# Prompt attention in pairs of heads on the halves of the matmul array, with half of the output projection between the units

## What is computed

```python
def _sparse_attend(q, ks, vs, valid):
    logits = jnp.einsum('bqhd,bqkhd->bqhk', q, ks).astype(jnp.float32) * (ATT_DIM ** -0.5)
    logits = jnp.where(valid[:, :, None, :], logits, -jnp.inf)
    p = jax.nn.softmax(logits, axis=-1).astype(vs.dtype)
    return jnp.einsum('bqhk,bqkhd->bqhd', p, vs)
...
    y = jnp.concatenate([att.reshape(B, T, ATT_WIDTH), jax.nn.silu(g) * retn], axis=-1)
    return y @ w_out
```

## Time and profile before

| | |
|---|---|
| median of 3 runs | 1618.3 us (1616.56 to 1624.8) |
| profiled execution | 1621.1 us, its span 1619.3 us |
| PE busy | 1528.2 us, 94% of the span |
| DVE, ACT, POOL busy | 567.3, 427.7, 193.3 us |
| mean granted clock of TensorE | 0.922 of 2.4 GHz |

### The profile page before, as it was taken

How to read it: one execution, slowest core, us unless ns; L and a number is a source line. 1 busy time by engine, 2 the same in 40 slices (tenths; PEclk the granted TensorE clock), 3 DMA queues, 4 the chain that set the end, 5 groups by cost and what they waited for, 6 DMA issues and landing times.

```text
span 1619.3 us, 27331 instructions
## 1 busy us (share of the span) xinstructions
PE 1528.2 (94%) x10150; PEld 1275.8 (79%) x10150; DVE 567.3 (35%) x1102; ACT 427.7 (26%) x686; POOL 193.3 (12%) x309
## 2 busy tenths in 40 slices
PE   6999999999999999999887689999989999999995
PEld 6999999999876477777532365556869999999995
DVE  3233333222412589802122354431153332332224
ACT  3334333221312200003110003331073343332123
POOL 0000000233131022220242110000140000000001
PEclk9999999999999999999998755557999999999998
DMA  4222222333222388873677420000202222222231
GB/s 185 79 91 79 90 80 88 89 105 96 75 70 93 110 257 256 260 247 126 196 254 243 126 104 1 0 1 27 78 28 90 91 83 86 91 87 72 84 94 56
DMA packets 65352, 176.76 MB, mean 109 GB/s; under 512 B 9682, under 2 KB 13779, under 8 KB 65043
## 3 DMA queue, kind: packets, MB, share of 16 engines
q1 hardware_dynamic: 49874, 131.30, 25.5%
q0 software_dynamic: 14560, 40.96, 8.0%
q10 hardware_dynamic: 864, 3.80, 0.6%
HBM read 169.00 MB, written 7.02 MB: 109 GB/s over the span
## 4 chain that ended last, share of the span: by engine, by line
PE 85%; DMA 4%; DVE 4%; issue 3%; ACT 3%; POOLq 1%; SPq 1%; POOL 1%; ACTq 0%; DVEq 0%
PE ps L347 82%; PE ps L350 3%; DMA dring<-in_v_pool 2%; DMA dring<-in_k_pool 1%; ACT xbuf L788 1%; DMA xbuf<-in_x_t 1%; POOLq L226 1%; DVE rbuf L1084 1%; DVE scr L1093 1%; ACT x_high L788 1%; ACT scr L788 1%; POOL dring L233 0%; DVE w_low L1023 0%; SPq L226 0%; DVE big L1084 0%
## 5 line engine op out<-in xcount | busy, mean ns | idle before, releaser
L347 PE MATMUL ps<-x_high,w_high 128*128 128x280 f32 (+1 forms) x1408 | 414.1, 294 | 18.3 <-DVE x_low L1029 11.0
L347 PE MATMUL ps<-x_high,w_low 128*128 128x280 f32 (+1 forms) x1408 | 411.5, 292 | 0.0
L347 PE MATMUL ps<-x_low,w_high 128*128 128x280 f32 (+1 forms) x1408 | 411.2, 292 | 0.0
L1023 DVE TENSOR_TENSOR w_low<-wring,w_high 128x1024 fp32r<-128x1024 f32 (+1 forms) x136 | 163.1, 1199 | 509.4 <-ACT w_high L788 509.3
L347 PEld LDWEIGHTS ps<-x_high,w_high 128*128 128x128 f32 x1408 | 268.2, 191 | 23.4 <-issue 13.5
L347 PEld LDWEIGHTS ps<-x_low,w_high 128*128 128x128 f32 x1408 | 268.2, 190 | 0.0
L347 PEld LDWEIGHTS ps<-x_high,w_low 128*128 128x128 f32 x1408 | 267.7, 190 | 0.0
L347 PE MATMUL ps<-xbuf,wring 128*128 128x280 f32 x1056 | 262.6, 405 | 1.2 <-ACT aux L788 0.9
L788 ACT ACTIVATE w_high<-wring 128x1024 fp32r<-128x1024 f32 (+1 forms) x136 | 140.7, 1035 | 423.4 <-PE ps L347 422.7
L347 PEld LDWEIGHTS ps<-xbuf,wring 128*128 128x128 f32 x1056 | 197.6, 191 | 58.2 <-issue 10.2
L347 PE MATMUL ps<-h_high,w_low 128*128 128x280 f32 (+1 forms) x704 | 203.8, 289 | 0.0
(11 more groups left out here) (170 smaller groups left out, 1325.6 us busy)
## 6 DMA issues: line engine op xcount, KB each, us to landing
wring<-in_wg SPq DMA_DIRECT2D x44, 512.0 KB, 3.5
wring<-in_wu SPq DMA_DIRECT2D x44, 512.0 KB, 3.4
wring<-in_w_in SPq DMA_DIRECT2D x33, 512.0 KB, 4.3
wring<-in_wd SPq DMA_DIRECT2D x32, 512.0 KB, 3.6
dring<-in_k_pool POOLq DMA_DIRECT2D x64, 256.0 KB, 3.6
dring<-in_k_pool SPq DMA_DIRECT2D x64, 256.0 KB, 3.3
dring<-in_v_pool POOLq DMA_DIRECT2D x64, 256.0 KB, 4.1
dring<-in_v_pool SPq DMA_DIRECT2D x64, 256.0 KB, 4.1
```

The costliest lines, as they stand in the source:

```text
L347: return nc.tensor.matmul(out, lhs, rhs, start=start, stop=stop, **kw)
L1023: v.tensor_tensor(wl[:, to, 0:n], w4[:, s, 0:n], wh[:, to, 0:n].bitcast(F32), ALU.subtract) \
```

## The change

Units become pairs: heads 2 hp and 2 hp + 1 for one tile, 16 of them. The two heads' scores are issued one behind the other, on rows 0 to 63 and 64 to 127 of the array, into PSUM banks 0 and 1, which are no longer used in turn. The values are issued in alternation, one head to partitions 0 to 63 and the other to 64 to 127 of one bank. The transposes stay as many as before, head after head. On DVE one instruction, `tensor_tensor_reduce`, adds the mask, multiplies by minus the scale and leaves the row minimum, so that the maximum and the negation go; for t=3 a second one covers the last 16 keys and a minimum joins the two. ACT copies both heads' turned blocks in one instruction, and DVE takes over the copy to `mix`, one for both heads.

The retention blocks (4 to 7) of the output projection become `ret_part`, one column half of one output block at a time, 16 parts of 4 matmuls, one in each round of the loop between scores and values. DVE adds each to alpha * x in place. The projection behind the attention is left with blocks 0 to 3. The weights of d = 4 to 7 now have a place of their own, the ring of the pages (`out_weight`), and SP loads them once the retention state has been written out.

In the diff below the removed functions, which are printed above, and the moved buffers are left out.

```diff
--- before.py
+++ after.py
...
@@ -320,8 +327,9 @@
             sp.wait_ge(sem("dst_full"), NB)
             for s in range(4):
                 weight(s, w_out[s])
-            for s in range(4):
-                weight(s, w_out[s + 4])
+            sp.wait_ge(sem("st_out"), 16 * NB)
+            for d in range(4, KT):
+                sp.dma_start(out_weight(d), w_out[d]).then_inc(sem(f"wo_in{d}"), 16)
             ffn_loads(1)
             for a in range(2):
                 with sp.Fori(0, KT) as i:
...
@@ -721,56 +729,84 @@
                 pe.wait_ge(sem("so_att"), g + 1)
                 tr(ps[0:64, 3, g * P:(g + 1) * P], so_rows[g], 0, P).then_inc(sem("so_turned"), 1)
 
...
+            pairs = [(hp, t) for hp in range(4) for t in TILES]
+
+            def scores(u, hp, t):
+                nk = min(SEEN[t], 512)
+                if u:
+                    pe.wait_ge(sem("al_done"), u)
+                qk = [(z[64 * h:64 * h + 64, Q + hp, real(t):real(t) + P], z[64 * h:64 * h + 64, K + hp, :]) for h in range(2)]
+                for h, (q, k) in enumerate(qk):
+                    last = mm(ps[:, h, 0:nk], q, k[:, 0:nk])
                 if t == 3:
...
+                    if u >= 4:
+                        pe.wait_ge(sem("apt_done"), u - 3)
+                    for h, (q, k) in enumerate(qk):
+                        last = mm(ps[:, 2, META * h:META * (h + 1)], q, k[:, 512:PL])
+                        if h == 0:
+                            last.then_inc(sem("tail_full"), 1)
+                            pe.wait_ge(sem("tail_full"), u // 4 + 1)
                 last.then_inc(sem("as_full"), 1)
 
...
+            def turn(u, hp, t):
                 pe.wait_ge(sem("ap_done"), u + 1)
...
+                if u:
+                    pe.wait_ge(sem("apt_done"), u)
+                for h in range(2):
+                    l = l_b[u % 3][:, h, :]
+                    for j in range(t + 1):
+                        tr(ps[:, 4 + h, j * P:(j + 1) * P], l[:, real(j):real(j) + P], 0, P)
+                    last = tr(turned_meta(t)[:, h, :], l[:, 0:META], 0, P)
+                last.then_inc(sem("at_full"), 1)
+
+            def values(u, hp, t):
+                pt_, bank = pt_b[u % 2], 6 + u % 2
                 pe.wait_ge(sem("apt_done"), u + 1)
                 if u >= 2:
                     pe.wait_ge(sem("ao_done"), u - 1)
...
+                for j in range(-1, t + 1):
+                    for h in range(2):
+                        o, hc = ps[64 * h:64 * h + 64, bank, 0:P], slice((2 * hp + h) * AD, (2 * hp + h + 1) * AD)
+                        if j < 0:
+                            last = mm(o, vtl[0:META, hc], pt_[0:META, h, (t + 1) * P:(t + 2) * P], True, False)
+                        else:
+                            last = mm(o, vt[:, j, hc], pt_[:, h, j * P:(j + 1) * P], False, j == t)
                 last.then_inc(sem("ao_full"), 1)
 
...
+            def ret_part(i):
+
+                d, a = divmod(i, 2)
+                if a == 0:
+                    if d < 4:
+                        weight(d)
+                    else:
+                        pe.wait_ge(sem(f"wo_in{d}"), 16)
+                if i:
+                    pe.wait_ge(sem("fill_done"), i)
+                for k in range(4, KT):
+                    last = mm(ps[:, 3, 0:HW[1]], out_weight(d)[:, k * P:(k + 1) * P], mix[:, k, cols(a, 1)], k == 4, k == KT - 1)
+                last.then_inc(sem("fill_full"), 1)
+
+            scores(0, *pairs[0])
             pe.wait_ge(sem("so_done"), 4)
...
+            for u in range(len(pairs) + 1):
+                if u + 1 < len(pairs):
+                    scores(u + 1, *pairs[u + 1])
+                if u < len(pairs):
+                    ret_part(u)
+                if u >= 1:
+                    values(u - 1, *pairs[u - 1])
+                if u < len(pairs):
+                    turn(u, *pairs[u])
+            pe.wait_ge(sem("ao_done"), len(pairs))
 
             for d in range(KT):
-                weight(d % 4)
                 pe.wait_ge(sem("r_done"), KT + 1 + d + 1)
-                wide(d % 2, w4[:, d % 4, :], KT, mix, 1).then_inc(sem(f"w_free{d % 4}"), 1)
+                for a in range(2):
+                    for k in range(4):
+                        last = mm(ps[:, 2 * (d % 2) + a, 0:HW[1]], out_weight(d)[:, k * P:(k + 1) * P], mix[:, k, cols(a, 1)],
+                                  k == 0, k == 3)
+                last.then_inc(sem(f"w_free{d}" if d < 4 else "wo_done"), 1)
             norm(1)
             ffn(1)
 
...
@@ -966,33 +1002,28 @@
                     ev(so_b[0], ps[:, 4, :]).then_inc(sem("so_out"), 1)
                     act.wait_ge(sem("so_full"), 2)
                     ev(so_b[1], ps[:, 7, :]).then_inc(sem("so_out"), 1)
...
+            pairs = [(hp, t) for hp in range(4) for t in TILES]
+
+            def probs(u, hp, t):
+                for h in range(2):
+                    l = l_b[u % 3][:, h, 0:SEEN[t]]
+                    act.wait_ge(sem("al_done" if h else "nmx_done"), u + 1)
+                    ev(l, l, ACT.Exp, bias=nmx[:, u % 2, h:h + 1], scale=-1.0, accum_out=ssum[:, u % 2, h:h + 1]) \
+                        .then_inc(sem("ae_done"), 1)
+
+            def turned(u, hp, t):
+                w, pt_ = (t + 1) * P, pt_b[u % 2]
                 act.wait_ge(sem("at_full"), u + 1)
                 if u >= 2:
                     act.wait_ge(sem("ao_full"), u - 1)
...
+                ev(pt_[:, :, 0:w], ps[:, 4:6, 0:w])
+                ev(pt_[0:META, :, w:w + P], turned_meta(t)).then_inc(sem("apt_done"), 1)
+
+            for u in range(len(pairs) + 1):
+                if u < len(pairs):
+                    probs(u, *pairs[u])
+                if u >= 1:
+                    turned(u - 1, *pairs[u - 1])
             w_in_t = [Tally(sem(f"w_in{s}"), 16 * seen[1][s]) for s in range(4)]
             norm(1)
             act.wait_ge(sem("kvi_out"), 48)
...
@@ -1331,44 +1362,65 @@
                     v.tensor_copy(o, t[:, :, :, h2, :]).then_inc(sem("so_done"), 1)
 
 
...
+            pairs = [(hp, t) for hp in range(4) for t in TILES]
+
+            def logits(u, hp, t):
+                m, w = acc_ap(t), min(SEEN[t], 512)
                 dve.wait_ge(sem("as_full"), u + 1)
                 if u >= 3:
                     dve.wait_ge(sem("at_full"), u - 2)
...
+                for h in range(2):
+                    l, low = l_b[u % 3][:, h, :], nmx[:, u % 2, h:h + 1]
+                    last = v.tensor_tensor_reduce(l[:, 0:w], ps[:, h, 0:w], m[:, 0:w], -AD ** -0.5, 3e38, ALU.add, ALU.min,
+                                                  low if t < 3 else nmt[:, h, 0:1])
+                    if t == 3:
+                        last.then_inc(own.sem, 1)
+                        v.tensor_tensor_reduce(l[:, 512:PL], ps[:, 2, META * h:META * (h + 1)], m[:, 512:PL], -AD ** -0.5, 3e38,
+                                               ALU.add, ALU.min, nmt[:, h, 1:2]).then_inc(own.sem, 1)
+                        dve.wait_ge(own.sem, own.up(2))
+                        last = v.tensor_tensor(low, nmt[:, h, 0:1], nmt[:, h, 1:2], ALU.min)
+                    last.then_inc(sem("al_done" if h else "nmx_done"), 1)
+
+            def ret_part(i):
+
+                d, a = divmod(i, 2)
+                o = x[:, d, cols(a, 1)]
+                dve.wait_ge(sem("fill_full"), i + 1)
+                v.scalar_tensor_tensor(o, o, ALPHA, ps[:, 3, 0:HW[1]], ALU.mult, ALU.add).then_inc(sem("fill_done"), 1)
+
+            def scaled(u, hp, t):
+                dve.wait_ge(sem("ae_done"), 2 * u + 2)
+                seq(v.reciprocal(rcp, ssum[:, u % 2, :]))
+                for h in range(2):
+                    l = l_b[u % 3][:, h, 0:SEEN[t]]
+                    last = v.tensor_scalar(l, l, rcp[:, h:h + 1], None, ALU.mult)
+                last.then_inc(sem("ap_done"), 1)
+
+            def out(u, hp, t):
+                dve.wait_ge(sem("ao_full"), u + 1)
+                v.tensor_copy(mix[:, hp, real(t):real(t) + P], ps[:, 6 + u % 2, 0:P]).then_inc(sem("ao_done"), 1)
+
+            n = len(pairs)
+            for u in range(n + 2):
+                if u < n:
+                    logits(u, *pairs[u])
+                if 1 <= u <= n:
+                    ret_part(u - 1)
+                if u >= 2:
+                    out(u - 2, *pairs[u - 2])
+                if u < n:
+                    scaled(u, *pairs[u])
 
             for d in range(KT):
...
+                dve.wait_ge(*((sem(f"w_free{d}"), OUT_W[d] + 1) if d < 4 else (sem("wo_done"), d - 3)))
+                if d == 0:
+                    dve.wait_ge(sem("fill_done"), 2 * KT)
                 if d < KT - 1:
-                    v.scalar_tensor_tensor(halves(rs[1][:, d, live(1)]), halves(x[:, d, live(1)]), ALPHA, pair(d % 2, 1),
...
+                    v.tensor_tensor(halves(rs[1][:, d, live(1)]), halves(x[:, d, live(1)]), pair(d % 2, 1), ALU.add) \
+                        .then_inc(sem("r_done"), 1)
```

(18 more changed lines are left out.)

26 lines of the change are left out of this document (7 added, 19 removed).

## The result

The kernel after takes 1539.5 us (median of 4 runs, 1532.3 to 1543.8) against 1618.6 of the kernel before beside it: a ratio of 0.9501, interval 0.9456 to 0.9545. The forecast was 1532, range 1518 to 1568, so faster, 0.5% above the forecast.

The account below looks back on a forecast made before the run. PE's streaming was taken to bound the attention, at half clock, and the projection. From 1621.1 us, 57.2 came off the attention and 30.7 off the projection: 1533.2 for the profiled execution, stated as 1532; range 1518 to 1568.

Parts of the forecast that it names:

- The projection: Output projection behind the attention: without its retention half it keeps 28.8 of 59.5 us, 30.7 less.
- R: Retention half of the projection, moved into the attention: 16 steps of 1.80 us at full clock, 3.60 at half.
- S and V in halves: Attention scores (S) and values (V): two heads on array halves overlap, so a pair costs about one head's time.
- The sizes: Attention, four pairs: 15.3 us of stream, transposes (T) included, plus 16 gaps of 0.2, 18.5; stage 82.3 against 139.5.
- the ramp and the ends: Attention stage: 4 us for the first microseconds at half clock, 3 us for the ends, as before.
- The clock: TensorE in the attention: full-array work raises the granted clock from 0.50 to the upper level, bar the first pair.
- rival 1: The clock stays at half in the attention: stage 147 us, total 1600; chance 0.13.
- The unsteady clock: A clock that goes up and down in the attention: total about 1566 us; chance 0.06.
- DVE: Attention, widest pair: 4.2 us of DVE work, 5.0 at the scan's price, hidden behind PE's 5.6.
- Waits: Attention queues: PE's R waits at most 0.43 us, inside the DVE sum; the later second-half w_out loads cost nothing.
- Rivals 2 and 4: Halves do not overlap: with the clock risen 1554 us, chance 0.05; with it at 0.50 1641, slower, chance 0.03.
- rival 3: The fused mask instruction is slow, 2.3 us per mean tile, so DVE sets the attention's pace: 1560 us; chance 0.05.

Follow-up runs that it names:

- e3: Kernel after the change, with both heads' values on one column half, one head after the other, and two copies to mix: 1552.7 us, ratio 0.9563.
- a0: The kernel after the change, unaltered, run and profiled again: 1537.1 us, ratio 0.9479.
- e1: Kernel after the change, with the 16 retention parts run behind the attention instead of between the pairs: 1544.9 us, ratio 0.9528.
- e2: Kernel before, single heads, with one retention part in every second unit and the projection as after the change: 1570.3 us, ratio 0.9692.
- e5: e1 with both heads' values on one column half and the second head's scores waiting for the first's: 1588.6 us, ratio 0.9789.
- e7: e1 with both heads' values on one column half, scores still on two row halves: 1563.4 us, ratio 0.9637.
- e8: e1 with the second head's scores waiting for the first's, values still on two column halves: 1577.7 us, ratio 0.9731.
- e6: Kernel after the change, with every transpose of the probabilities done twice into the same place: 1549.3 us, ratio 0.9559.
- e4: Kernel after the change, with mask, maximum and negation as three instructions instead of the fused one: 1536.2 us, ratio 0.9468.

## Why the prediction was right, and which step was not

**The projection** (30.7 less): 29.5 us stand where 28.8 were worked out. Moving R out is plain stream, and the term was right.

**S and V in halves** held. The estimate of 1.6 for two column tiles, worked out from the 2.38 times that the Trainium skill (TensorE: Matmul & The Clock Gate, Part 3) gives for three, was too low here: the trace gives 1.99. e3 shows the same from the other side: with the values on one half, at a clock that stays up, the stage is 17 us longer. For S, two heads' 400 columns took 0.88 us, where one head took 1.63 at half the clock.

**The sizes.** The sum had 18.5 us per four pairs and 0.3 for the tail; 19.63 were measured. R (8.13; 7.19 and four gaps of 0.2 make 7.99) and T (3.65 against 3.76) were right. V is 4.24 against 3.76 and S 3.61 against 3.32; these are the two terms that were mis-sized. V loses 0.31 to 0.33 us in each block beside its stream, with 8 instructions or with 20, where 0.2 was taken. S loses 0.21 in three of its blocks, but 0.75 in that of t=3, which has the two tails and the wait between them: 0.3 was taken for this, and some 0.5 came. Over four rounds that is 4 x 0.83 = 3.3 us; the ramp and the ends gave 1.2 back (the stage is 84.4, not 82.3). Most of the distance from 1532 to the profiled 1543.8 is no term of the sum but the 7.9 us by which the attention began later. (The 1532 itself lies 1.6 above what the prediction's own 1533.2 and 2.8 give.) In a0, which began within 1 us of before, 1621.1 - 1537.1 = 84.0 us were saved.

**The clock, and the step that said too little.** "After the change S, V and R all fill the array, and R alone is 3.6 us of each pair": the upper level came, but the sentence does not say which of the three it needs. e1 shows that R is not needed, e2 that the pairs are not: each is enough alone. So rival 1 was not near: with R between the units no run's attention stayed at 0.50. The unsteady clock is what e5, e7 and e8 show, without R and without one or both kinds of filled halves. An estimate of what it costs: e5's stage has a mean clock of 0.73, so some 57 of its 105.2 us lie at 0.50, and at full clock those would take about half, 28 less; e1's 59.5 us at 0.96 give 2 likewise. So more than half of the 45.7 us between the two stages is the clock, and the rest is left for the values and scores one after the other. The Trainium skill (same page, Part 4) says that transposes do not bring the faster clock. No run here contradicts that, but e6, with twice as many, kept 1.00, so they did not hold it down beside R and filled halves.

**DVE** was rightly costed at nothing in time: e4 gives back 17.8 us of its work and the stage stays. **Waits**: inside a round none was seen, and the one at the end (1.37 us) stands in the 3 us of ends. The loads that now run into the first microseconds of the stage (0.94 of the DMA engines' time in 980 to 984) held up no matmul there. Rivals 2 and 4 fell with the factor of 1.99, rival 3 with 0.77 us for the fused instruction.

**R between the units** I had only as a mover of work. e1 shows its second worth: it covers ACT's copy of the turned blocks, 9.2 us of waits in e1, none in the round of after shown above.

## What to carry to other kernels

Where an engine is 98% busy at half its clock with half its array, pairing the halves is worth two factors, the overlap and the clock; price them apart, and try each part alone. Two ways to the same gain do not add up: pairs alone and R alone, each against before, save 76 and 51 us, both together 79 to 86. Look next for other matmuls on a quarter of the array; here eight blocks ahead of the attention were worth more than the whole fused mask.

## What the runs showed of the hardware that was not expected

Without R and with only part of the array filled, the granted clock stayed at neither level: e5 had 0.50, 1.00, 0.50 and 1.00 again within 90 us, with PE over 97% busy in both (25.43 of 26 us in its fast stretch, 18.81 of 19 in its slow one). Four matmuls of 32 columns side by side, at half clock, took 0.66 us for eight instructions where one after another took 1.92, a factor of 2.9. And f32 matmuls, each two instructions on PE, overlap across the column halves almost fully: the factor of 1.99 is theirs.
